# Prompt attention of a hybrid decoder step: the scores of two narrow places are issued one behind the other

## The reference, cut to what matters

```python
s = jnp.einsum('nbqcgd,nbscd->nbcgqs', qb, kc, preferred_element_type=jnp.float32) * (hd ** -0.5)
...
s = jnp.where(mask[:, None, None], s + bias, NEG)
p, m, den = _softmax_stats(s, sink)
o = jnp.einsum('nbcgqs,nbscd->nbqcgd', p.astype(vc.dtype), vc, preferred_element_type=jnp.float32)
o = o / jnp.transpose(den, (0, 1, 4, 2, 3))[..., None]
```

## Time and profile before

| | |
|---|---|
| median of 3 runs | 2279.35 us (2274.39 to 2280.62) |
| the profiled execution, its time | 2273.25 us |
| its span | 2271.5 us |
| prompt attention in it | 250 to 429 us |
| of that, narrow places behind the ramp | 262 to 340 us |

### The profile page before, as it was taken

How to read it: one execution, slowest core, us unless ns; L and a number is a source line. 1 busy time by engine, 2 the same in 40 slices (tenths; PEclk the granted TensorE clock), 3 DMA queues, 4 the chain that set the end, 5 groups by cost and what they waited for, 6 DMA issues and landing times.

```text
span 2271.5 us, 33486 instructions
## 1 busy us (share of the span) xinstructions
PE 2216.8 (98%) x13723; PEld 1994.1 (88%) x13723; DVE 962.6 (42%) x1694; ACT 658.6 (29%) x1294; POOL 138.1 (6%) x216
## 2 busy tenths in 40 slices
PE   7999999899999999999999999989999999999998
PEld 7999777677789989899898998889989899898996
DVE  5110487565543424334243345662423324243346
ACT  5111586444431203112031223441302213031121
POOL 1000230000120000000000003320000000000001
PEclk9999999999999999999999999999999999999999
DMA  5320400497321202012020133230202102021023
GB/s 169 96 79 19 158 28 6 149 387 244 112 93 38 66 10 74 29 45 65 9 74 28 46 93 111 90 112 19 75 0 74 49 25 69 5 74 46 28 92 117
DMA packets 127726, 176.15 MB, mean 78 GB/s; under 512 B 14157, under 2 KB 96261, under 8 KB 127500
## 3 DMA queue, kind: packets, MB, share of 16 engines
q1 hardware_dynamic: 121436, 170.05, 23.0%
q10 hardware_dynamic: 6192, 4.72, 0.7%
HBM read 156.40 MB, written 18.58 MB: 77 GB/s over the span
## 4 chain that ended last, share of the span: by engine, by line
PE 76%; DVE 2%; DMA 1%; ACT 1%; issue 1%; POOL 0%; DVEq 0%; SPq 0%; POOLq 0%; ACTq 0%
PE ps L1751 33%; PE ps L1731 33%; PE ps L2626 4%; PE ps L2575 1%; PE ps L2594 1%; DMA sa_kb<-cache_b_k 1%; PE ps L1406 1%; PE ps L1740 1%; PE ps L1427 1%; PE ps L1467 0%; PE ps L1448 0%; DVE m_xT_lo L2381 0%; PE ps L2646 0%; ACT sa_kT L1278 0%; DVE sa_pb L1323 0%
## 5 line engine op out<-in xcount | busy, mean ns | idle before, releaser
L1695 DVE TENSOR_TENSOR t_y<-t_y,ps 128x512 f32<-128x512 f32 x288 | 197.7, 687 | 626.5 <-PE ps L1751 626.3
L1751 PE MATMUL ps<-t_w_hi,t_h_hi 128*128 128x512 f32 x1152 | 449.7, 390 | 2.9 <-DVE t_h_hi L1672 2.2
L1751 PE MATMUL ps<-t_w_lo,t_h_hi 128*128 128x512 f32 x1152 | 448.4, 389 | 0.0
L1751 PE MATMUL ps<-t_w_hi,t_h_lo 128*128 128x512 f32 x1024 | 398.4, 389 | 0.0
L1731 PE MATMUL ps<-m_xT_lo,t_w_hi 128*128 128x384 f32 x1488 | 327.9, 328 | 0.0
L1731 PE MATMUL ps<-m_xT_hi,t_w_lo 128*128 128x384 f32 x1488 | 327.9, 328 | 0.0
L1731 PE MATMUL ps<-m_xT_hi,t_w_hi 128*128 128x384 f32 x1488 | 327.8, 328 | 0.0
L1626 ACT ACTIVATE t_relu<-ps 128x384 f32<-128x384 f32 (+1 forms) x192 | 87.9, 458 | 810.2 <-PE ps L1751 776.7
L1656 DVE TENSOR_TENSOR t_w_lo<-t_raw,t_w_hi 128x1024 fp32r<-128x1024 f32 x128 | 155.4, 1224 | 277.1 <-ACT t_w_hi L1614 276.7
L1751 PEld LDWEIGHTS ps<-t_w_hi,t_h_hi 128*128 128x128 f32 x1152 | 216.2, 188 | 50.9 <-DVE t_h_hi L1672 3.1
L1731 PEld LDWEIGHTS ps<-m_xT_hi,t_w_hi 128*128 128x128 f32 x1488 | 254.8, 188 | 1.1
(11 more groups left out here) (231 smaller groups left out, 2475.7 us busy)
## 6 DMA issues: line engine op xcount, KB each, us to landing
t_raw<-mlp_w SPq DMA_DIRECT2D x128, 512.0 KB, 4.1
sa_kb<-cache_b_k SPq DMA_DIRECT2D x40, 512.0 KB, 10.1
sa_vb_even<-cache_b_v SPq DMA_DIRECT2D x20, 512.0 KB, 6.5
sa_vb_odd<-cache_b_v SPq DMA_DIRECT2D x20, 512.0 KB, 7.1
in_raw<-attn_w_in SPq DMA_DIRECT2D x6, 1024.0 KB, 5.2
t_rows<-scratch_x SPq DMA_DIRECT2D x12, 512.0 KB, 5.8
qT<-x_prompt SPq DMA_DIRECT2D x8, 512.0 KB, 3.6
t_rows<-x_prompt SPq DMA_DIRECT2D x8, 512.0 KB, 3.4
```

What stands on the lines that cost most here:

```text
L1695: self.nc.vector.tensor_tensor(part, part, self.core.ps[:, 6 + n % 2, :], ALU.add).then_inc(self.part_added, 1)
L1751: mm = self.nc.tensor.matmul(self.core.ps[:, 6 + half, :], a[:, k, t * P:t * P + P], w[:, k, half * 512:(half + 1) * 512], start=(k == 0 a ...
```

## The change

Only the place of the score matmuls in PE's order changes. Where an even narrow place p has a narrow place p + 1 behind it, S(p + 1) is issued right behind S(p), at step 2p, and no more at step 2p + 2. No instruction is added or removed; the orders of DVE, ACT, POOL and SP are the same as before, and every wait names the same semaphore and value.

```diff
+    def scored_at(step):
+
+        u = step
+        if step >= U or step % 2:
+            return []
+        if not wide(u) and u + 2 < U and not wide(u + 2) and u % 4 == 0:
+            return [u, u + 2]
+        return [] if not wide(u) and u % 4 == 2 and not wide(u - 2) else [u]
+
...
         for step in range(STEPS):
-            if step < U and step % 2 == 0:
-                scores(step)
+            for u in scored_at(step):
+                scores(u)
             for batch in batches_at(step):
                 for n in batch:
                     turn(n)
```

## The result

The changed kernel took 2287.62 us (median of 18 runs, 2283.13 to 2291.02), the one before 2278.03 us beside it (2272.76 to 2284.02). The ratio is 1.0042, 95% interval 1.0034 to 1.0049: 9.6 us slower. The forecast was 2283.4, 4.1 us slower than the median known then, so the way was right and the size less than half. It gave a change within 0.3% a chance of 0.71; what came is beyond that, in the part that it gave 0.26. The profiled execution has a span of 2289.2 us; it stands at the upper end of the runs (2291.02), as that of before stood at the lower end, so the two spans differ by 17.7 us, more than the medians. In what follows the place where the difference arises is read from one stretch.

The account below looks back on a forecast made before the run. PE, ACT and DVE, all nearly busy, wait for one another in a ring in the narrow places. -1.6 + 8.7 - 3.0 = +4.1 us on the 2279.35 us median gives 2283.4 us, range 2276 to 2290.

Parts of the forecast that it names:

- part 2: At nine narrow single-batch places, PE would stall for a chain through DVE before S(p + 3): +8.7 us.
- the lost cover: At the nine single-batch places, the batch between S(p) and S(p + 1) no longer hides the DVE chain.
- Part 3: Shortly behind the new stalls, PE's old waits for ACT's copies at T21, T33, T43, T61 go: -3.0 us.
- Part 1: At eight two-batch places, one run of scores less saves PE tiling-mode switches: -1.6 us.
- Part 4: At the eight two-batch places, transposes right behind transposes cost 0; 3.7 us if ACT's copies are always late.
- the slow rival: DVE chain costs 8.7 us, ACT gives nothing back and is late at doubled batches: +10.8 us, 2290.1 us; chance 0.26.

Follow-up runs that it names:

- experiment 3: The changed kernel, 7 slots, with DVE's copy moved behind b(2p + 3) at the nine single-batch places; ratio 1.0023 to the kernel before.
- experiment 4: The changed kernel with both 14 narrow `probs` slots and DVE's copy moved later at the nine single-batch places; ratio 1.0007 to the kernel before.
- experiment 5: On top of experiment 4, reciprocals and takes also moved behind b(2p + 3) at the same nine places; ratio 1.0003 to the kernel before.
- experiment 2: The changed kernel with 14 `probs` slots of 512 columns for narrow halves in place of 7 of 1024; ratio 1.0040 to the kernel before.
- experiment 1: The kernel before with S(p + 1) issued right behind S(p) only at the nine single-batch places; ratio 1.0026 to the kernel before.
- experiment 6: The kernel before with S(p + 1) issued right behind S(p) only at the eight two-batch places; ratio 1.0029 to the kernel before.
- experiment 7: The kernel before with S(p) and S(p + 1) joined for odd p instead of even; ratio 1.0013 to the kernel before.
- experiment 9: As experiment 4, but with scores joined only from place 14 on; ratio 1.0012 to the kernel before.

## Why the prediction was right in its way and short in its size

- **What bounds it, and the mechanism (part 2): right.** The chain T, b(2p + 1), copy, two biases, S(p + 3) is in the rows of S(29), and experiments 3 to 5 shorten it link by link: 10.7, 5.4, 4.1 and 2.3 us of waits for `pa_least`, ratios 1.0042, 1.0023, 1.0007, 1.0003. With the waits of scores for POOL it is 10.7, 6.9, 4.1 and 4.2 us, so the last step is the weak one. Two sentences of it were too strong: the 7 slots alone are not the cause (experiment 2), and the lost cover was put at the wrong batch (experiment 1).
- **The size of part 2.** Forecast and measured stalls: S(11) 1.65 and 1.57; S(13) 0.9 and 1.34; S(19) 1.15 and 1.01; S(27) 0.3 and none; S(29) 1.8 and 2.25; S(37) 1.25 and 0.92; S(43) 1.35 and 1.28; S(9) 0.3 and none. These sum to 8.7 and 8.4. That they agree so well is in part luck: single terms are off by up to 0.45 us both ways, and S(13) and S(29) hold 1.0 us that the sum did not have (last section). What I had not looked for are stalls behind places with two batches or with the batch at the second place: S(17) 0.46, S(39) 0.71, S(45) 0.85, S(48) 0.27, 2.3 us. Ahead of S(17) stands a slow copy of the reciprocals on DVE (0.93 us at 277.98 where most take 0.43), 0.50 us that may be all of its wait; no experiment took it away. Besides, the idle time in brackets starts at the modelled end of the matmul before: S(42) starts at 333.33 and S(43) at 335.23, 1.90 apart where 0.46 is the pitch, a stall of 1.44 for a bracket of 1.28. Ten such are 1.6 us more. Measured: about 12.3 us in place of 8.7.
- **Part 3, the old waits given back: right in the sum**, -2.9 (3.8 to 0.9) against -3.0. By places it was not: T43 still waits 0.61, which should have gone, and the wait of 0.38 at T77, which should have stayed, went.
- **Part 1, the switches: right in the rows, not shown in the time.** In the changed kernel 12 products take 0.80 us to the transposes behind them (273.83 to 274.63) and 0.81 to the next scores (278.10 to 278.91), so leaving out a run of scores costs nothing else. But experiments 6 and 7, which save as many, were slower than the kernel before; only the account of experiment 6 speaks for the 1.6 us.
- **Part 4: 0 held for ACT, not for POOL.** The doubled batches did not wait for ACT's copies. "No wait" for the pieces that POOL splits was wrong, though it cost nothing in this kernel: at S(29) the query piece was done at 301.32 and PE was there at 300.85, but the wait for DVE covered it. Experiments 3 and 5 lay it bare, with waits of 1.48, 1.33 and 0.56 us for query pieces, and experiment 7 with 1.28 us for a key piece.
- **Left out of the sum: the clock.** I had it as a danger within the slow rival. Behind S(29)'s stall the granted clock fell from its upper to its lower level (2.4 and 1.2 GHz) and rose again within 4 us. Two windows of the changed kernel:

```profile
304.00:306.00 2.00, 2.00 (x14) 1.67 (x15) 0.39 (x1) 1.09 (x3) 0.00 (x0) 0.55 0.00 0
306.00:308.00 2.00, 2.00 (x19) 1.67 (x16) 1.18 (x7) 2.00 (x8) 0.32 (x1) 0.59 0.01 4
```

  Sixteen products take 1.97 us at 305.39 where they take 1.09 elsewhere. Four microseconds at 0.57 are 1.7 us of work lost, an estimate from these rows. The runs say the same without a trace: among the 18 of the changed kernel the time is about 1.8 us longer for each 0.001 less of mean granted clock, and their mean clock is 0.9927, while that of the kernel before beside the experiments is 0.9940 to 0.9944. By that, 2 to 3 of the 9.6 us are clock, an estimate.
- **The sum again**, for the profiled stretch: 12.3 of stalls, -2.9, -1.6, +1.7 of clock, is 9.5 us of the 10.3. It has -1.6 as forecast, which no time shows. The rest is within the ramp, where S(8) starts 0.7 us later (263.46 against 262.73) at half clock.
- **The chances.** The slow rival, +10.8 us, was nearest to what came, though its reasons were half wrong: ACT did give back what it owed, and the doubled batches did not wait for its copies. Its number came close by luck: 3.7 us for copies that nobody waited for stood in for stalls at other places and for the clock. I should have priced the stalls at all places by the same chain instead of at nine, and taken the interaction (every stall delays the T on which DVE waits next) as the likely case.

## What to carry to other kernels

Issuing work early on an in-order engine uses up the distance that hid another engine's latency; before moving it, follow the buffer it will write back to its last reader and see what that reader waits for in its own order. If that is work now queued behind the moved instruction, the move closes a ring. If such a move is wanted, the reader's order must be moved with it: here the joined scores cost 0.42% alone and nothing measurable once `probs` had 14 slots and DVE's copies, reciprocals and takes stood behind the biases that the scores need. Even so no order tried was faster than the one before. And loosen the links of such a ring together, too: of two that are equally long, one alone shows nothing (1.0040), which says nothing against the ring.

## What the runs showed of the hardware that was not expected

- **A stall of 2.25 us was followed by a granted clock of 0.55.** Waits of 1.48 to 1.60 us were followed by a fall in some kernels (experiment 9, 0.56 from 300 us; experiment 1, 0.55 from 268; experiment 3, 0.62 from 268) and by none in others (the changed kernel behind S(11)'s 1.57 us; experiments 4 and 6 behind S(29)'s 1.59 and 1.61). These rows give no rule by the length of the wait.
- **DVE's copy of the reciprocals takes 0.43 us, or up to 1.0.** It is a copy from SBUF to SBUF of fp32. In the changed kernel it took 1.00 us at 270.35 and 0.83 us at 300.76, and both times POOL's subtraction was running when it started:

```profile
270.33 0.73 POOL L944 TENSOR_TENSOR pa_q_lo<-qT,pa_q_hi 128x256 fp32r<-128x256 f32 x1 [2.87 <-ACT pa_q_hi L951]
270.35 1.00 DVE L1050 COPY pa_rden<-pa_rden_one 128x512 f32<-128x512 f32 x1
```

```profile
300.58 0.74 POOL L944 TENSOR_TENSOR pa_q_lo<-qT,pa_q_hi 128x256 fp32r<-128x256 f32 x1
```

  In both it ends 0.29 and 0.27 us behind the end of POOL's. Where no POOL operation overlaps it, it took 0.43 us. In the kernel before one started 0.07 us ahead of POOL's; there it kept its 0.43 us, and POOL's took 0.95 instead of 0.73 us:

```profile
296.88 0.43 DVE L1041 COPY pa_rden<-pa_rden_one 128x512 f32<-128x512 f32 x1
```

```profile
296.95 0.95 POOL L935 TENSOR_TENSOR pa_q_lo<-qT,pa_q_hi 128x256 fp32r<-128x256 f32 x1
```

  The two slow copies add 1.0 us to the chains of S(13) and S(29), the two stalls that exceeded their forecast. The Trainium skill (SBUF — State Buffer, Terms) says that DVE and GpSimd share one pair of ports and that the loser waits for the whole instruction. The trace agrees in both orders; that no other cause is at work was not tried by an experiment.
